# Two of four token tiles get all 16,384 expert scores from TensorE in place of gathered key rows

## The reference

```python
s1 = einsum('thd,kd->thk', q[..., :half], keys_1)    # 8 heads, 128 keys each
s2 = einsum('thd,kd->thk', q[..., half:], keys_2)
v1, i1 = top_k(s1, 16);  v2, i2 = top_k(s2, 16)
sc, ci = top_k((v1[..., :, None] + v2[..., None, :]).reshape(...), 16)
eidx = e1 * 128 + e2                                 # (T, 128): 128 experts per token
gates = softmax(sc)
act = gelu(einsum('td,tkd->tk', x, peer_u[eidx]))    # key rows, 1024 wide, 16384 of them
y = einsum('tk,tkd->td', gates * act, peer_v[eidx])  # value rows
```

## Time and profile before

| | us |
|---|---|
| median of 3 runs | 3099.1 (3094.14 to 3100.05) |
| the profiled execution, device time | 3098.76 |
| its span, first to last instruction | 3097.4 |
| TensorE busy with matmuls | 2260.3 |
| VectorE busy | 1795.0 |
| GpSimd busy | 1330.2 |
| ScalarE busy | 462.6 |
| mean granted TensorE clock | 0.802 of 2.4 GHz |

### The profile page before, as it was taken

The page is one execution under the profiler, slowest core; times in us unless marked ns, Lnnn a source line. Parts: engine busy times, 40 slices in busy tenths (PEclk is TensorE's granted clock), DMA queues, the critical chain, the costliest instruction groups (busy, mean ns, idle before and its releaser), DMA issues. The chain is left out here.

```text
span 3097.4 us, 24710 instructions
## 1 busy us (share of the span) xinstructions
PE 2260.3 (73%) x8222; PEld 1385.4 (45%) x8222; DVE 1795.0 (58%) x3876; ACT 462.6 (15%) x1305; POOL 1330.2 (43%) x1041
## 2 busy tenths in 40 slices
PE   5997982046692594777684578979957687969988
PEld 3545861023442472533343336758425343437543
DVE  1512017988878777777567996774656954223300
ACT  1201000001210100111100332012000321013310
POOL 0000001376767677666668763674665533100000
PEclk9886996568695696898785557989977699986999
DMA  3310431589889899978889876999998879942466
GB/s 124 131 63 33 150 114 57 172 301 389 311 302 355 308 402 369 376 291 319 327 285 389 310 258 229 391 374 400 359 367 328 281 259 392 343 148 90 147 248 223
DMA packets 291758, 829.56 MB, mean 268 GB/s; under 512 B 23568, under 2 KB 30016, under 8 KB 290864
## 3 DMA queue, kind: packets, MB, share of 16 engines
q0 software_dynamic: 148464, 539.99, 47.8%
q1 hardware_dynamic: 139872, 283.19, 25.3%
q10 hardware_dynamic: 3296, 4.80, 0.4%
HBM read 825.81 MB, written 2.10 MB: 267 GB/s over the span
## 5 line engine op out<-in xcount | busy, mean ns | idle before, releaser
L314 POOL DMA_INDIRECT picks_rows<-peer_u_dram,expert x512 | 701.8, 1371 | 858.9 <-DVE expert L1475 521.0
L314 POOL DMA_INDIRECT picks_rows<-peer_v_dram,expert x512 | 620.8, 1213 | 502.8 <-DVE h L380 346.5
L374 DVE CUSTOM_DVE_ANT_0 picks_rows<-picks_rows,xn 128x1024 f32<-128x1024 f32 x512 | 613.4, 1223 | 168.7 <-DMA picks_rows<-peer_u_dram,expert 148.7
L380 DVE SCALAR_TENSOR_TENSOR h<-picks_rows,picks_weight,h 128x1024 f32<-128x1024 f32 x416 | 533.4, 1282 | 153.5 <-DMA picks_rows<-peer_v_dram,expert 82.8
L465 PE MATMUL psum<-weight_ring,hnT 128*128 128x512 f32 (+4 forms) x576 | 236.4, 572 | 23.9 <-DMA weight_ring<-w_in_dram 11.9
L1763 PE MATMUL psum<-weight_ring,aT 128*128 128x512 f32 x512 | 220.8, 593 | 2.9 <-ACT aT L2070 1.4
L403 PE MATMUL psum<-picks_rows,picks_diag 128*128 128x512 f32 x384 | 172.0, 607 | 27.4 <-ACT picks_diag L332 24.3
L465 PEld LDWEIGHTS psum<-weight_ring,hnT 128*128 128x128 f32 (+1 forms) x576 | 105.8, 186 | 153.1 <-issue 137.4
L656 PE MATMUL psum<-identity_sb,n_scaled 128*128 128x128 f32 (+1 forms) x104 | 23.9, 409 | 183.6 <-DVE n_scaled L640 183.6
L1763 PEld LDWEIGHTS psum<-weight_ring,aT 128*128 128x128 f32 x512 | 97.0, 190 | 125.1 <-issue 120.5
L876 PE MATMUL psum<-identity_sb,na_probs 128*128 128x128 f32 (+2 forms) x384 | 92.5, 360 | 72.3 <-DVE na_probs L962 56.2
(11 more groups left out here) (353 smaller groups left out, 3193.4 us busy)
## 6 DMA issues: line engine op xcount, KB each, us to landing
weight_ring<-w_ff_dram SPq DMA_DIRECT2D x48, 2048.0 KB, 10.9
weight_ring<-w_in_dram SPq DMA_DIRECT2D x44, 2048.0 KB, 14.2
weight_ring<-w_proj_nsa_dram SPq DMA_DIRECT2D x6, 2048.0 KB, 8.5
weight_ring<-w_out_dram SPq DMA_DIRECT2D x6, 2048.0 KB, 14.6
weight_ring<-w_ret_out_dram SPq DMA_DIRECT2D x4, 2048.0 KB, 7.8
weight_ring<-w_mix_out_dram SPq DMA_DIRECT2D x4, 2048.0 KB, 18.7
weight_ring<-w_peer_q_dram SPq DMA_DIRECT2D x4, 2048.0 KB, 13.4
picks_rows<-peer_u_dram,expert POOLq DMA_INDIRECT x512, 7.5
```

The lines of the kernel that those rows point to most:

```text
L314: pool.indirect_dma_start(out=self.rows[:, n % GATHERS, :], out_offset=None, in_=table, in_offset=bass.IndirectOffsetOnAxis(ap=self.expert ...
L374: ins = nc.vector.tensor_tensor_reduce(out=row, in0=row, in1=self.x[t], scale=1.0, scalar=0.0, op0=ALU.mult, op1=ALU.add, accum_out=self.d ...
L380: ins = nc.vector.scalar_tensor_tensor(out=h, in0=row, scalar=self.weight[:, t % 2, k:k + 1], in1=h, op0=ALU.mult, op1=ALU.add)
```

## The change

For tiles 0 and 1, TensorE multiplies the normed tokens with the whole transposed key table (`peer_uT`, 32 slabs of 128 x 8 x 512, 2 MB each), ScalarE copies each 128 x 512 result from PSUM and stores it on its own DMA queue to a DRAM tensor `scores[t]` of 128 x 16384, and the 128 dots that a token needs are gathered back from there, one float per partition and gather. The new stage `ex` (`experts_stage`) holds both selections too, and takes the place of `sel0` and `sel1`. Tiles 2 and 3 gather key rows as before. No value row goes to TensorE any more, so `weigh`, `add`, `fold`, the diagonal matrices and the two banks are gone (`BANKS` 6 to 8). There are 768 row steps instead of 1024, and 256 gathers of single floats, issued by GpSimd too: the 128 of tile 0 in one go, once all scores are stored, those of tile 1 one after each value row of tile 0. `SHARES` is new: the first stage with steps is `ma3_1`, and `drain_0` has none.

```diff
-BANKS = 6
-V_BANKS = (6, 7)
+BANKS = 8
 SHARES = {
-    "sel1": 24, "n1_1": 13, "lat_1": 13, "nq_1": 9, "nkv_1": 9, "up_1": 12, "qk_1": 16, "tq_1": 6, "tk_1": 5, "ma2_1": 26,
-    "ma3_1": 27, "rp_1": 35, "tr_1": 7, "re_1": 58, "rn_1": 9, "m1_1": 55, "mix_1": 18, "np_1": 22, "pq_1": 18, "sel2": 51,
-    "sel3": 51, "drain_0": 28, "n22_0": 11, "u2_0": 7, "pool2_0": 11, "q2_0": 14, "kc2_0": 9, "kv2_0": 15, "cmp2_0": 41,
-    "tq2_0": 7, "tk2_0": 3, "na2_0": 81, "m2_0": 46, "out2_0": 14, "n32_0": 11, "ff12_0": 50, "ff22_0": 49, "nf2_0": 11,
-    "n22_1": 4, "u2_1": 3, "pool2_1": 5, "q2_1": 5, "kc2_1": 3, "kv2_1": 4, "cmp2_1": 24, "tq2_1": 3, "tk2_1": 1,
-    "na2_1": 35, "m2_1": 10, "out2_1": 3, "n32_1": 5, "ff12_1": 11, "ff22_1": 12, "nf2_1": 4}
+    "ma3_1": 10, "rp_1": 22, "tr_1": 3, "re_1": 17, "rn_1": 4, "m1_1": 41, "mix_1": 12, "np_1": 5, "pq_1": 12, "sel2": 65,
+    "sel3": 89, "n22_0": 10, "u2_0": 7, "pool2_0": 9, "q2_0": 14, "kc2_0": 8, "kv2_0": 13, "cmp2_0": 30, "tq2_0": 7,
+    "tk2_0": 3, "na2_0": 74, "m2_0": 42, "out2_0": 13, "n32_0": 10, "ff12_0": 45, "ff22_0": 45, "nf2_0": 10, "n22_1": 5,
+    "u2_1": 4, "pool2_1": 5, "q2_1": 6, "kc2_1": 3, "kv2_1": 5, "cmp2_1": 22, "tq2_1": 3, "tk2_1": 2, "na2_1": 40,
+    "m2_1": 12, "out2_1": 4, "n32_1": 5, "ff12_1": 14, "ff22_1": 13, "nf2_1": 5}
 GATHERS = 8
-DIAGS = 8
+STAGES = 4
+SCORED = (0, 1)
...
+        if first in SCORED:
+            one += [(("pu", c), a["peer_uT"][c], n) for c in range(SLABS)]
...
+    def issue_scored(self, pool, tiles, stored):
+        for signal in stored:
+            pool.wait_ge(*signal)
+        self.gather_scores(pool, tiles[0], range(PICKS))
+        for t in tiles:
+            for k in range(PICKS):
+                self.gather_row(pool)
+                if t + 1 in tiles:
+                    self.gather_scores(pool, t + 1, range(k, k + 1))
...
+            pool.indirect_dma_start(
+                out=self.dots[:, t % 2, k:k + 1], out_offset=None, in_=self.scores[t],
+                in_offset=bass.IndirectOffsetOnAxis(ap=self.place[:, t, k:k + 1], axis=0),
+            ).then_inc(self.dots_landed[t], 16)
...
     def activate(self, act, turn=None):
         limit = self.last if turn is None else self.after(turn)
+        while self.activated < NT and self.values_at[self.activated] < limit:
+            t = self.activated
+            if t in SCORED:
+                act.wait_ge(self.dots_landed[t], 16 * PICKS)
+            else:
+                act.wait_ge(self.taken, self.values_at[t])
+            if t:
+                act.wait_ge(self.weight_ready, t)
+            self.g.nc.scalar.activation(self.active[:], self.dots[:, t % 2, :], ACT.Gelu).then_inc(self.active_ready, 1)
+            self.activated += 1
...
+def experts_stage(g, tag, names, tiles, xnT, pqT, room, tables, expert, place, gates):
...
+    next_keys, next_exp = SLABS // 4, SLABS // 2
...
+        def tensor(pe):
+            g.begin(pe)
+            for c, name in enumerate(names):
+                if c == 0:
+                    keys(pe, 0)
+                if c == next_keys and n > 1:
+                    keys(pe, 1)
+                w = g.w.view(name)
+                g.w.arrived(pe, name)
+                for j in range(n):
+                    i = n * c + j
+                    if i >= 4:
+                        pe.wait_ge(*s_copied.after(i - 3))
+                    for k in range(KT):
+                        mm = nc.tensor.matmul(bank(i), xnT[:, k, P * j:P * j + P], w[:, k, :], start=(k == 0), stop=(k == KT - 1))
+                    mm.then_inc(g.w.products_done, 1)
...
+                    nc.scalar.copy(staged[:, i % STAGES, :], bank(i)).then_inc(s_copied.sem, 1)
+                    act.wait_ge(*s_copied.after(i + 1))
+                    rows = g.picks.scores[t].rearrange("(p e) o -> p (e o)", p=P)
+                    act.dma_start(rows[:, 512 * c:512 * c + 512], staged[:, i % STAGES, :]).then_inc(s_stored[i % STAGES].sem, 16)
...
+            for i, signal in enumerate(s_stored):
+                act.wait_ge(*signal.after(16 * len(range(i, n * SLABS, STAGES))))
+            exponentials(act, n - 1)
```

More of the change, by code:

```diff
@@ L266, with __init__ @@
 class Picks:
-    def __init__(self, g, ctx, peer_u, peer_v, expert, gates):
+    def __init__(self, g, ctx, peer_u, peer_v, scores, expert, place, gates):
         nc, self.g = g.nc, g
@@ L297, in after, with end @@
     def after(self, turn):
[L298 removed]
         return self.first + (self.last - self.first) * min(turn, self.turns) // self.turns
[L301 to L303 removed]
+    def end(self, t):
+        return self.values_at[t] + PICKS
     def issue(self, pool, t):
[L307 removed]
         pool.wait_ge(self.expert_ready, t + 1)
[L309 to L318 removed]
@@ L335, in activate, with gather_row @@
+    def gather_row(self, pool):
+        n = self.issued
+        t, kind, k = self.steps[n]
+        if n >= GATHERS:
+            pool.wait_ge(self.taken, n - GATHERS + 1)
+        pool.indirect_dma_start(
+            out=self.rows[:, n % GATHERS, :], out_offset=None, in_=self.peer_u if kind == "key" else self.peer_v,
+            in_offset=bass.IndirectOffsetOnAxis(ap=self.expert[:, t, k:k + 1], axis=0),
+        ).then_inc(self.landed[n % GATHERS], 16)
+        self.issued += 1
     def activate(self, act, turn=None):
@@ L381, in use_to @@
                                                      op1=ALU.add)
-            ins.then_inc(self.taken["dve"], 1)
-    def add(self, pe, turn=None):
-        self.add_to(pe, self.last if turn is None else self.after(turn - 1))
-    def add_to(self, pe, end):
-        nc = self.g.nc
-        while self.added < end:
-            n = self.added
-            self.added += 1
-            if self.owner[n] != "pe":
-                continue
-            t, _, k = self.steps[n]
-            at = self.number[n] - 1
-            mine = [m for m in range(PICKS) if on_pe(t, m)]
-            if k == mine[0] and self.sums[t]:
-                pe.wait_ge(self.sum_added, self.sums[t])
-            pe.wait_ge(self.landed[n % GATHERS], 16 * (n // GATHERS + 1))
-            pe.wait_ge(self.diag_ready, at + 1)
-            for c, bank in enumerate(V_BANKS):
-                mm = nc.tensor.matmul(self.g.psum[:, bank, :], self.diag[:, at % DIAGS, :],
-                                      self.rows[:, n % GATHERS, 512 * c:512 * c + 512], start=(k == mine[0]), stop=(k == mine[-1]))
-            mm.then_inc(self.taken["pe"], 1)
@@ L900, in tensor @@
                 value(pe, s - lag - 1)
-                g.picks.add(pe, 2 * min(s, steps))
-            g.picks.add(pe)
         def exponentials(act, s):
@@ L1816, in first_wave @@
     local = lambda t: slice(P * (t - first), P * (t - first) + P)
-    expert, gates, state = rooms["expert"], rooms["gates"], rooms["state"]
+    expert, place, gates, state = (rooms[x] for x in ("expert", "place", "gates", "state"))
     kT, v, tables = rooms["kT"], rooms["v"], rooms["tables"]
@@ L2072, in second_wave @@
     rows = a["out"].rearrange("(t p) d -> p t d", p=P)
-    norm_stage(g, tag("nf"), [(g.h[:, t, :], P, None) for t in tiles], D, token_out=g.picks.x[first:last],
+    norm_stage(g, tag("nf"), [(g.h[:, t, :], P, None) for t in tiles], D, token_out=[rooms["xn"][:, t, :] for t in tiles],
                gain_rows=tables["g_final"], store=[rows[:, t, :] for t in tiles])
```

300 lines of the change are left out of this document (177 added, 123 removed).

## The result

The changed kernel took 3342.3 us (median of 4 runs, 3333.25 to 3353.23) against 3099.15 (3094.14 to 3100.05): ratio 1.0784, interval 1.0752 to 1.0817. The forecast was 3350. The profiled execution took 3353.23 with a span of 3351.9 us at a mean granted clock of 0.821.

The account below looks back on a forecast made before the run. TensorE was taken to bound the first wave, row steps the second, with stages as barriers. Terms 312.5 - 146.3 + 160 - 45.9 - 28 = +252.3 on 3098.76 gave 3351.1, stated as 3350 us, range 3285 to 3430.

Parts of the forecast that it names:

- Term 1: Stage `ex`: 32 slabs at 13.76 us on TensorE; second wave begins at 926.5 us, not 614.0: +312.5 us.
- Term 2: Second wave, `n1` to `pq`: first 107 steps gone, GpSimd's issues set the end at 1448 us: -146.3 us.
- cheap-gather rival: Second wave: narrow gathers nearly free, `ma3` doesn't stall, value rows at old pace: -61 us, 3290; chance 0.07.
- The lock of VectorE and GpSimd: Second wave: the two engines can exclude each other; at worst 126 steps take 476 us, not 355, some 120 more.
- the 145 packets a gather: Second wave: any gather width has one descriptor per partition, 145 packets each, so a narrow gather is priced as a row.
- Term 3: `sel2` and `sel3`: VectorE does every step, 103 more values at 1.28 us and 24 keys at 1.15: +160 us.
- Term 4: `drain_0` is empty: -45.9 us.
- Term 5: Second block: 340 steps instead of 380 in its first wave, 148 instead of 132 in tile 2's: -28 us.

Follow-up runs that it names:

- Experiment 2: Changed kernel with one plain load of 128 consecutive scores per token and tile in place of its 256 narrow gathers: 3252.4 us, ratio 1.0474.
- first series: The first four runs of the unaltered changed kernel, chip not on record: 3342.3 us, ratio 1.0784 against the kernel before.
- Experiment 3: Kernel before without TensorE's 96 value rows: no scored tile, all 1024 row steps on VectorE; 3164.7 us, ratio 1.0166.
- experiment 6: Changed kernel with TensorE's 96 value rows of tile 1 back and plain loads in place of the narrow gathers: 3218.9 us, ratio 1.0348.
- Experiment 11: Repeat of the changed kernel with 8 value steps moved from `sel3` to the drain, beside the unaltered one on the same chip: 3475.1 us, ratio 1.1181.
- 1: Changed kernel with each product of `ex` summing 4 of the 8 slices of the width: 3254.7 us, ratio 1.0489.
- experiment 4: Changed kernel with TensorE's 96 value rows of tile 1 back, 3 staging buffers instead of 4: 3443.8 us, ratio 1.1065.
- 8: Changed kernel with 8 of tile 1's value steps moved from `sel3` to the drain: 3467.9 us, ratio 1.1141.
- experiment 9: The changed kernel itself, unaltered, measured again in a later series on chip 8: 3473.2 us, ratio 1.1169.
- experiment 12: Changed kernel scoring tile 0 through all slabs first, then tile 1, each slab loaded twice, tile 0's gathers under the scoring: 3460.5 us, ratio 1.1108.
- 5: Changed kernel with half-depth scoring and plain loads in place of the 256 narrow gathers: 3032.8 us, ratio 0.9751.
- 7: Changed kernel with TensorE scoring tile 0 only, tile 1's key rows gathered early, TensorE's 96 value rows kept: 3154.0 us, ratio 1.0145.
- experiment 10: Changed kernel with 8 steps moved to the drain and a GpSimd fill after each of tile 0's 128 narrow gathers: 3424.2 us, ratio 1.1017.

## Why the prediction was right, and where it was not

**Term 1** (+312.5): measured +313.1, `ex` over at 927.1 us. The form of `ff22_0` gave its time to 0.4 us (440.4 against 440.0), DMA share 0.51 at 184 GB/s, no slab late.

**Term 2** (-146.3): measured -128.1. The mechanism is right: dots late in `ma3` (wait 48.4, forecast 44), first value step 1096.1 (forecast 1090), GpSimd and not the stages sets the end. From 1091 to 1466.8 us it made 257 issues at 1.10 us, 0.30 after each, which is the 1.41 taken from `sel2`. `pq` ended at 1466.8, not 1448: GpSimd started 4 us later, made five more issues and waited 16 us for VectorE. Experiment 2 confirms it by taking the gathers away: -90 us against the first series, where the cheap-gather rival had said -61. The lock of VectorE and GpSimd that I weighed from the Trainium skill ("SBUF — State Buffer", "two separate sides") would have made it 476 us for 252 issues. The trace has 376 for 257, so it doesn't bite at each step. There the Trainium skill sets the lock only against a GpSimd instruction that reads SBUF, a condition that I had left out; no run here tells whether an indirect DMA's issue is one. One reading under the price was wrong and cost nothing: the 145 packets a gather hold for rows only. The program has 119,824 packets on the gathers' queue, and 111,632 in experiment 2 without the 256 narrow gathers, so a narrow gather has 32. GpSimd took almost a row's time for it all the same.

**Term 3** (+160): the term that was mis-sized; measured +124.2 (`sel2` and `sel3` 297.8 us in place of 173.6). I charged each added step its full duration, though the windows of before held 34 us of VectorE waits. Experiment 3 measured the same rule by itself, 58 us for 96 rows (perhaps 12 of them a hold-up of TensorE), and experiment 6 its reverse, -33.5.

**Term 4** (-45.9): measured -36.8. The drain hid the second block's table loads, and with it empty nothing does. I did not ask what an empty stage had covered. Timeline of ScalarE and its queue after the last gates (1764.12 us):

```profile
1764.48 0.34 ACTq L1902 DMA_DIRECT2D pe_sb<-pe_table_dram  x1
...
1769.27 0.49 ACTq L1902 DMA_DIRECT2D w_sb<-w_cv_dram  x1
1773.76 1.06 ACT L574 ACTIVATE n_squares<-h 128x1024 f32<-128x1024 f32 x1 [24.68 <-DMA w_sb<-w_cv_dram]
```

Some 9 us from the last gates to the first square. Experiment 11 got 6.7 back.

**Term 5** (-28): measured -17.9. `ff22_0` is unchanged, as said.

The misses (T2 +18.2, T4 +9.1, T5 +10.1, T1 +0.6 against T3 -35.8) nearly cancel: +2.2 us. That the sum came out this close is partly luck.

**What it did not have at all** is the standstill. I priced the narrow gather by what it takes of GpSimd, and asked who waits for its result, but not what an unbroken run of 128 of them does to engines that don't wait for it. In the first series it did nothing that the profile shows (`lat_1` to `tk_1` 80.9 us, forecast 81). In every later run with the burst (experiments 1, 4, 8, 9, 11, 12) TensorE fell to one instruction in 1.40 us. In those with no stretch of more than 10 gathers 1.25 us apart (2, 5, 6) it did not. Some shorter stretches of other gathers have short hold-ups beside them: 18 row gathers in 3, and rows and narrow gathers in turn in 7 and 10. Shown: the burst is the cause of the long standstill (1 against 5, 4 against 6, with 8 for the chip), it follows the gathers in time (12), and spacing the gathers by a fill removes it (10). The program does not decide (9 against the first series). Not shown: that narrowness matters at all; experiment 3 speaks against it, and no run has a long burst of row gathers. Open: what is short of what, and why the first series escaped, though its burst begins with 48 gathers at the same pace; all that differs there is the chip or the moment, and which of them was not tried. The kernel before is 7 to 19 us slower in the later series than in the first. If the forecast were held against the later series, it would be 123 us too low.

## What to carry to other kernels

A gather of one float per partition costs GpSimd nearly as much as a gather of 4 KB (1.04 us against 1.21), so work that replaces row gathers by narrow gathers relieves VectorE and the DMA queues but keeps GpSimd the bound. An added step costs only what exceeds the waits of its stage, and a stage that is emptied may have hidden loads: count both before summing. Don't issue a long unbroken run of gathers from GpSimd beside work on other engines; space them, and time a kernel that has one on more than one chip before its number is believed.

## What the hardware did that I had not expected

- Beside the burst (one gather each 1.25 us) TensorE issues one instruction each 1.40 us, in the dense products of experiment 12 as in the short ones of `lat_1`, and in experiment 12 until 14 us after the last gather. At one gather each 1.59 us (experiment 10) it does not. An estimate of the onset from when the second product of `lat_1` is copied (due 947.6 us, copied at 955.6, each slow instruction 1.24 us longer than at the usual pace): 6 to 7 instructions before the due time, near 946.6 us, 20 us or 16 gathers into the burst. The same sum gives 20 us for experiments 1, 4 and 8. In 11 and 12 the first late copy is only 2 us late, and the slow pace holds for good only somewhat later.
- TensorE's records run ahead of its work. In experiment 9 some 68 records, 35 matmuls and 33 weight loads, start between that onset and the first slow start near 956 us. The Trainium skill ("PSUM — Partial Sum Buffer", "Engine vs sequencer instructions") gives TensorE a queue 64 deep; the trace agrees in size, if the records are taken at the entry to it. A hold-up of TensorE is then dated by who waits for its products, not by its own records.
- The trace's record of the instruction queue (q8 on the page) has one packet of 16 KB for about 256 instructions of TensorE. In experiment 9 there is one at 944.9 us and the next at 1152. Since the records of starts run on for 68 instructions after completions are already late, the missing packets look like a consequence of the hold-up and not its cause. The first series has a packet at the same place, 945.0 us, and no hold-up, so that packet alone doesn't start one. That is argued and not tested.
- The granted clock falls to 0.50 to 0.54 in the hold-up, with TensorE nearly idle. It follows the hold-up and isn't its cause: from 940 to 955 us of experiment 4, where completions are already late, it is still 1.00.
